# A mixture-of-experts entry taken apart: router and shared block per tile, shared downs inside the first four quads, gather operand without stride

## The reference

```python
def hier_moe(h, w_rg, b_rg, w_re, b_re, w_gate, w_up, w_down, ws_gate, ws_up, ws_down, w_sg):
    # router: top-1 of 8 groups by xt @ w_rg + b_rg, then top-2 of the 8 experts in it
    # each chosen expert e: (silu(xb @ w_gate[e]) * (xb @ w_up[e])) @ w_down[e], times its gate
    ...
    ys = (jax.nn.silu(xt @ ws_gate) * (xt @ ws_up)) @ ws_down
    y = y + jax.nn.sigmoid(xt @ w_sg) * ys
```

## Time and profile before

| | us |
|---|---|
| median of 3 runs | 3034.23 (3033.41 to 3039.97) |
| the profiled execution | 3026.92 |
| its span | 3025.1 |
| TensorE busy | 2607.5 (86%) |
| VectorE busy | 846.8 (28%) |
| ScalarE busy | 426.7 (14%) |
| queue q1 (all weight loads) | 690.00 MB, 60.0% of 16 engines' span |
| clock granted over the span | 0.95 |

### The profile page before, as it was taken

One profiled execution on the slowest core, in us unless ns is written; L12 is line 12 of the kernel. 1 busy time (PEld: TensorE's weight loads), 2 busy tenths in 40 slices (PEclk: granted clock), 3 DMA queues, 4 the chain that ended last, 5 costly groups with the idle time before them and its releaser, 6 DMA issues.

```text
span 3025.1 us, 34067 instructions
## 1 busy us (share of the span) xinstructions
PE 2607.5 (86%) x13714; PEld 1460.8 (48%) x13714; DVE 846.8 (28%) x1782; ACT 426.7 (14%) x794; POOL 203.1 (7%) x267
## 2 busy tenths in 40 slices
PE   5996887699999998899979988878879988788886
PEld 3443444444444445544467443434367854443443
DVE  3143635720021016410033311111157642111111
ACT  1031211120010012210010100000023421000001
POOL 3111101120000002010010100000000010000000
PEclk9998999799999999999989999999989999999998
DMA  6547458543444353054562599999943055999997
GB/s 239 204 162 263 170 194 304 180 145 130 166 160 161 131 179 119 25 201 139 196 204 79 217 417 421 421 421 421 399 134 126 6 208 207 410 421 421 421 421 300
DMA packets 264855, 721.87 MB, mean 239 GB/s; under 512 B 15248, under 2 KB 149040, under 8 KB 210864
## 3 DMA queue, kind: packets, MB, share of 16 engines
q1 hardware_dynamic: 251232, 690.00, 60.0%
q0 software_dynamic: 13520, 30.41, 3.1%
HBM read 719.17 MB, written 1.18 MB: 238 GB/s over the span
## 4 chain that ended last, share of the span: by engine, by line
PE 66%; DMA 21%; DVE 7%; SPq 2%; ACT 2%; issue 2%; POOL 0%; DVEq 0%; ACTq 0%; POOLq 0%
PE ps L887 23%; DMA ring<-in_moe_w_up 17%; PE ps L1511 9%; PE ps L994 7%; PE ps L912 5%; PE ps L1096 4%; PE ps L1078 3%; DMA ring<-in_ada_w 3%; SPq L544 2%; PE ps L1050 2%; PE ps L1615 2%; PE ps L923 1%; PE ps L1451 1%; PE ps L892 1%; PE ps L1281 1%
## 5 line engine op out<-in xcount | busy, mean ns | idle before, releaser
L887 PE MATMUL ps<-ring,hT 128*128 128x512 f32 x1632 | 720.5, 596 | 16.3 <-ACT hT L1741 12.2
L887 PEld LDWEIGHTS ps<-ring,hT 128*128 128x128 f32 x1632 | 307.0, 191 | 382.1 <-issue 363.7
L1511 PE MATMUL ps<-arena 128*32 128x512 f32 x1536 | 264.7, 675 | 85.1 <-DMA ring<-in_moe_w_up 80.7
L1511 PE MATMUL ps<-ring,arena 128*32 128x512 f32 x512 | 264.0, 676 | 0.0
L1501 PEld LDWEIGHTS ps<-arena,h 128*128 128x128 f32 x1024 | 248.4, 334 | 15.2 <-issue 11.6
L1501 PE MATMUL ps<-arena,h 128*128 128x128 f32 x1024 | 244.9, 398 | 3.4 <-issue 3.4
L994 PE MATMUL ps<-ring,arena 128*128 128x512 f32 x528 | 232.2, 593 | 2.4 <-ACT arena L1807 2.4
L2281 DVE SCALAR_TENSOR_TENSOR arena<-ps,arena 128x256 f32<-128x256 f32 x66 | 28.0, 425 | 578.9 <-ACT arena L1803 578.6
L1511 PEld LDWEIGHTS ps<-arena 128*32 128x32 f32 x1536 | 65.8, 121 | 256.8 <-issue 170.6
L912 PE MATMUL ps<-hT,ring 128*128 128x256 f32 x768 | 172.4, 387 | 2.5 <-ACT hT L1741 1.5
L1050 PE MATMUL ps<-ring,cond 128*2 128x128 f32 (+1 forms) x3072 | 106.5, 299 | 68.0 <-DMA ring<-in_ada_w 63.0
(11 more groups left out here) (530 smaller groups left out, 2434.6 us busy)
## 6 DMA issues: line engine op xcount, KB each, us to landing
ring<-in_moe_w_down SPq DMA_DIRECT2D x128, 1024.0 KB, 17.6
ring<-in_ada_w SPq DMA_DIRECT2D x48, 2048.0 KB, 13.1
arena<-in_moe_w_gate SPq DMA_DIRECT2D x96, 1024.0 KB, 11.9
arena<-in_moe_w_up SPq DMA_DIRECT2D x96, 1024.0 KB, 10.1
ring<-in_ffn_w_in SPq DMA_DIRECT2D x66, 1024.0 KB, 9.0
ring<-in_ffn_w_out SPq DMA_DIRECT2D x33, 1024.0 KB, 5.0
ring<-in_moe_w_gate SPq DMA_DIRECT2D x32, 1024.0 KB, 15.9
ring<-in_moe_w_up SPq DMA_DIRECT2D x32, 1024.0 KB, 17.9
```

The source lines that it names most:

```text
L887: m = pe.matmul(o3, lhsT_of(k), ring[:, a:a + 2, k * EH:(k + 1) * EH], start=start and k == 0, stop=stop and k == KC - 1)
L1511: m = pe.matmul(ps[a * CAP:(a + 1) * CAP, 6, :].rearrange("p (u c) -> p u c", u=2), x_slots[:, k, a * CAP:(a + 1) * CAP], slot_pair(gate_s ...
```

## The change

- The last add of the norm (L2238) writes the rows of the experts' stage not to `h` but to `h_routed`, a part of `hT`, with the eight interleaved column sets laid out as runs. Transposes and gather read contiguous runs there in place of `h[:, t, k::KC]`.
- TensorE's order is: transposes, router and block (0,0) of tile 0, then transposes, router and block (0,1) of tile 1; ranks; block (1,0), first turn, a wait for the first turned rows' copy, block (1,1); then quad 0. The second turn comes inside quad 0, behind its gather.
- The four shared downs are done inside quads 0 to 3 (`meanwhile`), ahead of the wait for `quad_hid`. Their weights have places of their own (`h`, which is free now, half of `x_sb`, and `junk`), loaded by SyncE in four pieces of 512 KB after router 1.
- The first four quads are written out, the other twelve stay in a loop.
- The four sums are opened by ScalarE, which copies zeros into PSUM.
- Slots of the shared weights: 1 to 4 in the first layer, 0, 1, 3, 4 in the second; downs of experts 0 and 3 are loaded early where their slots are free. In the second layer `gdn_out` uses slots 2 to 5, and the first shared weights are issued ahead of `experts_ahead`.

```diff
+        SHARED_DOWN = [[h[:, 0, :], h[:, 1, :]], [x_sb[:, 1, :], junk[:, :]]]
+        SHARED_SLOT = [[(1, 2), (3, 4)], [(0, 1), (3, 4)]]
+        PEELED = 2
+        h_routed = [hT[:, :, t * P:(t + 1) * P] for t in range(2)]
...
+                n.align()
                 b0 = n.block
-                mlp(2, lambda i: shared[i])
+                for i in range(2):
+                    for part in range(2):
+                        fill(SHARED_SLOT[l][i][part], shared[i][part])
+                    if i == 0 and ahead is not None:
+                        ahead()
+                early = [a for a in (0, 3) if DOWN_SLOT[a] not in SHARED_SLOT[l][0]]
+                for a in early:
+                    fill(DOWN_SLOT[a], I["moe_w_down_2"][l, a].rearrange("(p j) n -> p (j n)", j=2))
+                n.block += 4
+                sp.wait_ge(block_done, b0 + 1)
+                for i in range(2):
+                    wd = I["shared_w_down_2"][l][i * EH:(i + 1) * EH, :].rearrange("(p j) n -> p j n", j=2)
+                    for j in range(2):
+                        sp.dma_start(SHARED_DOWN[i][j], wd[:, j, :]).then_inc(sem("shared_down_loaded"), 16)
...
             def moe(l):
-                norm_tiles(LAT, open_sums)
...
+                router(0)
+                shared_gate_up(l, 0, 0, free)
+                router(1)
+                shared_gate_up(l, 0, 1, free)
...
+                shared_gate_up(l, 1, 0, gu0 + 1)
+                shared_turn(0, gu0 + 2)
                 pe.wait_ge(sem("rounds_known"), l + 1)
-                shared_turn(1, gu0 + 4, tp0)
-                shared_down(1, tp0)
+                rounds = pe.value_load(rounds_i[0:1, 0:1], min_val=1, max_val=SEQ // CAP)
+                pe.wait_ge(sem("sums_opened"), 4 * (l + 1))
+                pe.wait_ge(tp_evacuated, tp0 + 1)
+                shared_gate_up(l, 1, 1, gu0 + 2)
...
-                            m = pe.matmul(ps[:, 4 + k // 4, (k % 4) * P:(k % 4 + 1) * P], h[:, t, k::KC], sel[:, t, :],
+                            m = pe.matmul(ps[:, 4 + k // 4, (k % 4) * P:(k % 4 + 1) * P], h_routed[t][:, k, :], sel[:, t, :],
                                           start=t == 0, stop=t == 1)
                     m.then_inc(S("gathered"), 1)
+                    if turn:
+                        shared_turn(1, n.gu)
...
+                    if meanwhile is not None:
+                        shared_down(l, *meanwhile)
                     pe.wait_ge(S("quad_hid"), c + 1)
...
-                with pe.Fori(0, QUADS // 2) as qq:
+                for q in range(2 * PEELED):
+                    landed = landed_by(q // 2, q % 2)
+                    with pe.If(rounds > 1):
+                        with pe.Fori(1, rounds) as r:
+                            one_round((rounds * q + before if q else before) + r - 1, q % 2, landed, first=q == 0)
+                    one_round(rounds * (q + 1) + before - 1, q % 2, landed, True, first=q == 0, turn=q == 0, meanwhile=divmod(q, 2))
+                with pe.Fori(PEELED, QUADS // 2) as qq:
...
+                for b in range(4):
+                    tell(nc.scalar.copy(ps[:, b, :], zero_t[:, :]), sem("sums_opened"))
...
+                if routed:
+                    k_runs = lambda v: v.rearrange("p (q k) -> p k q", k=KC)
+                    tell(V.tensor_tensor(h_routed[t - 2], k_runs(h[:, b, :]), k_runs(v_shift[:, :]), ALU.add), h_ready)
```

More of the change, by code:

```diff
@@ L571, in experts @@
                 gate_up_load(UP_SLOT[3], I["moe_w_up_2"][l, 3])
+                for a in (0, 3):
+                    if a not in early:
+                        down_load(DOWN_SLOT[a], I["moe_w_down_2"][l, a])
                 sp.wait_ge(block_done, b0 + 4)
@@ L933, in norm_turned, with routed_turned @@
                     transposes([h[:, b, 4 * half + kk::KC] for kk in range(4)])
+            def routed_turned(t):
+                n.h += 1
+                pe.wait_ge(h_ready, n.h)
+                for half in range(2):
+                    transposes([h_routed[t][:, 4 * half + kk, :] for kk in range(4)])
             def norm_tiles(tiles, between=None):
@@ L1448, in shared_down @@
                 for t in range(2):
                     for half in range(2):
[L1450 to L1454, removed]
-            def moe(l):
-                norm_tiles(LAT, open_sums)
[L1458 to L1461, removed]
+                        pe.matmul(ps[:, 2 * t + half, :], hidT[:, i, j, t * P:(t + 1) * P],
+                                  SHARED_DOWN[i][j][:, half * 512:(half + 1) * 512],
+                                  start=False, stop=False, skip_group_check=True)
@@ L1493, in moe, with one_round @@
                 rounds_before[0] = rounds
-                def one_round(c, parity, landed, last=False):
+                def one_round(c, parity, landed, last=False, first=False, turn=False, meanwhile=None):
                     gate_slot = GATE_SLOT[parity]
+                    if first:
+                        pe.wait_ge(gu_evacuated, n.gu)
                     pe.wait_ge(S("sel_ready"), c + 1)
@@ L2050, in moe @@
             def moe(l):
+                n.block += 2
                 for t in range(2):
[L2052 removed]
                     n.gu += 1
@@ L2099, in one_round @@
                     nc.scalar.copy(z_slots[:, 0:512], ps[:, 4, :]).then_inc(S("z_lo"), 1)
-                with act.Fori(0, QUADS) as q:
+                with act.If(rounds > 1):
+                    with act.Fori(1, rounds) as r:
+                        one_round(r + before - 1)
+                one_round(rounds + before - 1, True)
+                with act.Fori(1, QUADS) as q:
                     with act.If(rounds > 1):
@@ L2237, in norm_tile @@
                                           op0=ALU.mult, op1=ALU.mult))
-                tell(V.tensor_tensor(h[:, b, :], h[:, b, :], v_shift[:, :], ALU.add), h_ready)
+                if routed:
+                    k_runs = lambda v: v.rearrange("p (q k) -> p k q", k=KC)
+                    tell(V.tensor_tensor(h_routed[t - 2], k_runs(h[:, b, :]), k_runs(v_shift[:, :]), ALU.add), h_ready)
+                else:
+                    tell(V.tensor_tensor(h[:, b, :], h[:, b, :], v_shift[:, :], ALU.add), h_ready)
                 n.h += 1
@@ L2785, in moe @@
                 for t in range(2):
-                    src = gu_next()
-                    tell(V.tensor_tensor(logits[:, t, :], src[:, 0:ROUTE_W], route_b, ALU.add), gu_evacuated)
-                for t in range(2):
+                    dve.wait_ge(block_done, n.block + 2 * t + 1)
+                    tell(V.tensor_tensor(logits[:, t, :], ps[:, t, 0:ROUTE_W], route_b, ALU.add), gu_evacuated)
                     choose(l, t)
+                n.gu += 2
+                n.block += 2
                 sg0, tp0 = tell.told.get("sig_seen", 0), n.tp
```

115 lines of the change are left out of this document (55 added, 60 removed).

## The result

| | before | after |
|---|---|---|
| median | 3033.82 us (4 runs, 3032.55 to 3039.97) | 3001.32 us (4 runs, 2994.22 to 3004.50) |
| the profiled execution | 3026.92 | 3001.57 |
| its span | 3025.1 | 2999.8 |
| TensorE busy | 2607.5 (86%) | 2520.6 (84%) |
| clock granted over the span | 0.95 | 0.927 |

The ratio is 0.989, with a 95% interval from 0.9872 to 0.9909: 32.5 us faster between the medians, 25.3 us between the two profiled executions. The forecast was 9 us faster, with a range that ended at 3003. The sign was right and, as the runs show, so were the two mechanisms (a shorter way into each stage, and a loop that loses time by the clock); the size was too small by more than a factor of three. Of all executions that follow, one of `e2_before_filled` (3107.53 us, granted clock 0.903) lay in a slower state of the chip; the ratios leave it out.

The account below looks back on a forecast made before the run. Expert stages were taken as bound by weight transfers once running, by the way in until then. Ways in -29.1 us plus 20 given back in the loop made -9.1, from median 3034.23 to 3025 us; range 3003 to 3037.

Parts of the forecast that it names:

- The way in, layer 0: Path to the end of quad 0's gate and up products in the first layer: 12.0 us gained (1735.6 to 1723.6).
- The shared weights are issued only at 1660.45: Layer 0: weights land late, so block (0,0) starts near 1668.3 behind a 4 us pause, plus 1.7 us for low clock.
- Block (1,1)'s wait for the first turned copy: Layer 0: block (1,1) waits 2.4 us for ScalarE's table load, sigmoid and copy, running 1.5 us later than before.
- Bare cover: Sigmoid, hidden product and quad 0's selection, until now hidden by the shared downs, lie bare before the gather: 4.0 us.
- Layer 1: Way into the second layer's expert stage: quad 0 frees its slots at 2532.5 against 2551.2, 18.7 us gained.
- VectorE's strided rows: VectorE writes tile 1's rows with a strided read: between 0 and 1.2 us more each layer, 0.5 taken.
- The loop: Over 15 quads and two layers, longer TensorE pauses lower the clock and starve the transfers: 20 us given back.
- X: Time of a quad's gate and up products (L1511): 8.35 us mean before, 9.1 taken after, up to 10.3.
- the constant of the ring: Issue, transfer, product, issue takes 21.5 us plus product time, against 29.87 of transfers; keeps up only below about 8.4.
- The transfer to the median: Profiled execution 3026.92 against median 3034.23: the forecast difference was taken over unchanged to the median, giving 3025 us.
- Rival A: In the loop the flow does not starve, so only the way in counts: 3005 us, chance 0.2.
- Rival C: No change: way in gives less, through jumps of written-out quads (3.4 us a layer) and low clock: 3035, chance 0.12.

Follow-up runs that it names:

- e2_before_filled: The kernel before with three products of zeros by zeros added after each gather: 3028.20 us against 3031.31, ratio 0.9985.
- e5_shared_late: The changed kernel with SyncE's first shared weights held, in the first layer only, until the mixer's last product is done: 3008.96 us against 3001.21.
- e7_filled_less: The changed kernel with five products of zeros after the gather in the loop's quads, none in quads 1 to 3: 2990.32 us, again 2990.41 (ratios 0.9870, 0.9855).
- e9_filled_uneven: The changed kernel with two products of zeros in the loop's even quads, six in odd, none in quads 1 to 3: 2988.73 us, ratio 0.9851.

## Why the prediction was wrong

The median came out 24 us below the forecast: 16 us in the profile's account (7.1 and 2.9 on the ways in, 6.3 in the loops) and 7 us from the step from profile to median.

**The way in, layer 0: 12.0 us forecast (11.2 with what was set off for strided writes and waits), 18.3 measured, 19.9 counted from tile 0's transposes.** This is the step that failed: "The shared weights are issued only at 1660.45". It took the old slots' release for the new ones. The mixer's output weights lie in slots 3, 4, 5 and 0 in the first layer, not in 0 to 3, so slots 1 and 2 are free early, which is what they were picked for. Counted from the transposes, block (0,0) began at 4.8 us and not at the forecast 8.6, without the 1.7 for the low clock, and block (1,0), next behind the ranks, at 24.3 and not at 29.6: 5.4 us, the largest part of what was missed. `e5_shared_late` puts the price of late weights at 8.6 us on the way in and 7.8 us of kernel time. ("The ranks follow at 1689.3, against 1690.0" sets them against the start of block (1,0), 1689.98; the ranks of the kernel before start at 1688.92. The gain of 12.0 does not hang on it.) The counter `n.pos` would have told: 33 units, then 12, leave it at 3.

**Block (1,1)'s wait for the first turned copy: 2.4 us forecast from block to copy, 1.2 measured.** The new wait was seen; that ScalarE's earlier wait for the round count would pull the table load ahead of the block was not. A step that is moved takes with it what stands behind it in its queue, and here that was a gain.

**Bare cover: 4.0 us forecast, 3.2 measured** (1700.81 to 1704.03). Right. The low clock in the gather after it, 1.7 forecast, was 5.44 - 3.75: right here, but it is no fixed price. Behind the same pause (3.04 to 3.05 us) the gather took 3.81 us in `e7_filled_less` and 6.66 in `e9_filled_uneven`. The gather without stride: 3.6 forecast, 3.83 measured in the second quad, 3.73 in most others.

**Layer 1: 18.7 us (17.9) forecast, 20.8 measured.** The term for filling the wait for tile 1 was right (5.7: ranks at 2503.14 before, and 2485.41 + 12.12 carried over = 2497.5). Of the 2.1 above the forecast 1.2 is the table load again; the bare cover (a pause of 2.61 us) gives most of the rest.

**VectorE's strided rows: 0.5 us taken, between 0 and 1.2 given; 2.01 us in place of 1.22 measured**, and hidden in part.

**The loop: 20 us given back forecast, 13.7 measured.** The mechanism is shown by three runs (the gather alone, and both fillings): right. The product's time, 9.1 taken, was 9.29 and 8.94: right. (That X is 8.73 to 8.77 in all quads but one of four was misread: one more of the four is 8.5. The mean stands.) What was off is the constant of the ring, 21.5 us. It was read off quad 1, where the load landed 18.1 us after its issue; in the starved loop one landed after 17.1. From the end of a product to the start of the next are 20.1 to 21.7 us in the last nine spacings of each stage, 20.7 and 20.8 in the mean. With 20.8 the ring's edge is near 9.1 and not 8.4, and 0.3 and 0.5 us a quad are lost there, not 0.7. A part of the 13.7 is not this ring at all: 3.8 us are at the entry of the loop. There "before L1511 of quads 1 to 3 they hide in the pause" leaves out quad 4, and the shared downs, taken as covered ("where TensorE then pauses 3 to 7 us for the load anyway"), lie on the path in quad 3. The filled kernels, with loops of 900.7 to 906.2 us, are still above the 893.4 of the kernel before with filling, in part for the filling itself, which is on the path at that entry.

**The transfer to the median: 7 us.** The prediction carried the difference over unchanged. The profiled execution of before (3026.92) was below every other run of that kernel (3027.15 to 3039.97), that of after in the middle of its own. It was a lucky one, and that was visible: profile 3026.92, median 3034.23. That a ring on its edge, which the clock can tip, makes such luck is argued and not shown. Filling the pause of the kernel before gives 3 us, but the profiles show another source too: 8 us between the earliest and the latest start of tile 0's transposes in the changed kernel's profiles, with the same code ahead of them. How the 7 us divide stays open.

Rival A (the flow does not starve, 3005) was nearest to the time, for a wrong reason: the flow did starve. Rival C's jumps exist, five or six of them, and are hidden but for one in the first stage and two in the second. The Trainium skill's advice to leave the ramp of the clock out ("TensorE: Matmul & The Clock Gate", Part 1) does not hold in this kernel: the filling gives back 11 us of 3001, under its one per cent, yet a third of what the change brings.

## What to carry to other kernels

Sum the ring, not only the transfers: from the issue of a load to its landing, the product that frees its slot, and back; if the sum equals the transfers of a turn, any engine that gets slower by a microsecond starves the queue, though its idle time looks like slack. Shortening off-path work in such a loop may lengthen a pause of TensorE and lower its clock in just the product on the path; cheap products of zeros in the pause bring back what it cost (2989 to 2993 us here, against 3001). And when buffers are moved, take the release times of the slots they go to from the allocator's counter, not from the rows of the old ones.

## What was unexpected of the hardware

TensorE's granted clock can be held by work that has no effect. Three products of zeros by zeros in the 3 us pause of the kernel before kept all 30 gate and up products of quads 1 to 15 at 7.1 us, where 23 of them took 8.5 to 8.8; seven in the longer pause of the changed kernel kept 23 of 30 there, for a mean of 9.29 and 8.94 without them. The same pause of 3 us did not always bring the same low clock behind it (gathers of 3.81, 5.44 and 6.66 us). A wait of 2.4 to 3.2 us, shown as nothing, appears at jumps over code that is not run (3.4 us in all before, 16.3 after).
